# Moving the causal convolution of a hybrid block: 8 of 31 taps on TensorE as 32x32 diagonal blocks behind the attention heads, 23 on VectorE begun by channel pairs

## The reference

```python
h = rms_norm(x, mix_norm)
a, g, q, k, v, fl = jnp.split(h @ w_in, splits, axis=-1)      # 512 each, fl: 8
# convolution part, 512 channels
u = a * jax.nn.sigmoid(g)
y = depthwise causal convolution of u with 31 taps + conv_b
y_conv = silu(layer_norm(y))
# attention part: 8 heads of 64, with a decay from log_sigmoid(fl)
p = softmax(q k^T / 8 + cum[i] - cum[j], masked to j <= i)
y_attn = p v
x = x + concat(rms_norm(y_conv), rms_norm(y_attn)) @ w_out
```

## Time and profile before

| | |
|---|---|
| median of 3 runs | 1214.56 us (1214.38 to 1214.64) |
| the profiled execution | 1214.71 us, span 1213.0 us |
| granted TensorE clock | 0.999 of full speed (2.4 GHz) |
| PE busy | 1200.2 us (99%), 6271 matmuls |
| DVE busy | 783.7 us (65%) |
| ACT busy | 618.3 us (51%) |
| POOL busy | 66.6 us (5%) |
| first mixer, from a in rows to the start of `mix_out` | 194.0 to 286.7 us in the span |

### The profile page before, as it was taken

How to read it: one execution, slowest core, us unless ns; L and a number is a source line. 1 busy time by engine, 2 the same in 40 slices (tenths; PEclk the granted TensorE clock), 3 DMA queues, 4 the chain that set the end, 5 groups by cost and what they waited for, 6 DMA issues and landing times.

```text
span 1213.0 us, 15892 instructions
## 1 busy us (share of the span) xinstructions
PE 1200.2 (99%) x6271; PEld 1023.7 (84%) x6271; DVE 783.7 (65%) x940; ACT 618.3 (51%) x792; POOL 66.6 (5%) x130
## 2 busy tenths in 40 slices
PE   8999999999999999999999999999999999999998
PEld 6888888998888888899998888888888888888886
DVE  4766546797655554778887755564678666565545
ACT  5544426675544443565744544543556755445333
POOL 1000002002000000200001000000014000000000
PEclk9999999999999999999999999999999999999999
DMA  8987764451587765545302587775365437886630
GB/s 272 314 282 252 237 209 154 153 189 43 174 279 236 257 227 190 186 161 175 123 1 70 164 280 250 242 251 192 138 210 200 147 116 242 255 258 228 230 137 35
DMA packets 172306, 235.32 MB, mean 194 GB/s; under 512 B 13800, under 2 KB 127560, under 8 KB 172232
## 3 DMA queue, kind: packets, MB, share of 16 engines
q1 hardware_dynamic: 172232, 234.30, 59.4%
HBM read 221.67 MB, written 12.58 MB: 193 GB/s over the span
## 4 chain that ended last, share of the span: by engine, by line
PE 90%; DVE 7%; ACT 1%; POOL 1%; DMA 0%; issue 0%; SPq 0%; DVEq 0%; ACTq 0%; POOLq 0%
PE bank L1656 27%; PE bank L1658 27%; PE bank L1657 27%; DVE y L1202 3%; DVE wlo L1085 2%; PE bank L1690 1%; PE bank L2070 1%; PE bank L2085 1%; PE bank L2028 1%; PE bank L2021 1%; PE bank L2093 1%; DMA raw<-in_ffn_w_dram 0%; PE bank L2190 0%; PE bank L2212 0%; PE bank L2177 0%
## 5 line engine op out<-in xcount | busy, mean ns | idle before, releaser
L1085 DVE TENSOR_TENSOR wlo<-raw,whi 128x2048 fp32r<-128x2048 f32 (+1 forms) x190 | 416.1, 2194 | 242.6 <-ACT whi L438 242.6
L438 ACT ACTIVATE whi<-raw 128x2048 fp32r<-128x2048 f32 x190 | 363.0, 1915 | 222.2 <-PE bank L1658 213.4
L1656 PE MATMUL bank<-whi,xThi 128*128 128x512 f32 x1024 | 402.0, 393 | 2.7 <-DVE xTlo L1598 1.3
L1658 PE MATMUL bank<-whi,xTlo 128*128 128x512 f32 x1024 | 399.0, 390 | 0.0
L1657 PE MATMUL bank<-wlo,xThi 128*128 128x512 f32 x1024 | 398.6, 389 | 0.0
L1656 PEld LDWEIGHTS bank<-whi,xThi 128*128 128x128 f32 x1024 | 192.3, 188 | 43.5 <-DVE xTlo L1598 2.0
L1658 PEld LDWEIGHTS bank<-whi,xTlo 128*128 128x128 f32 x1024 | 192.2, 188 | 40.1
L1657 PEld LDWEIGHTS bank<-wlo,xThi 128*128 128x128 f32 x1024 | 192.4, 188 | 39.0
L1656 PE MATMUL bank<-whi,hThi 128*128 128x512 f32 x352 | 137.3, 390 | 0.0
L1658 PE MATMUL bank<-whi,hTlo 128*128 128x512 f32 x352 | 137.0, 389 | 0.0
L1657 PE MATMUL bank<-wlo,hThi 128*128 128x512 f32 x352 | 137.0, 389 | 0.0
(11 more groups left out here) (411 smaller groups left out, 1083.9 us busy)
## 6 DMA issues: line engine op xcount, KB each, us to landing
raw<-in_ffn_w_dram SPq DMA_DIRECT2D x176, 256.0 KB, 4.3
raw<-in_ffn_w_in_dram SPq DMA_DIRECT2D x176, 256.0 KB, 4.1
raw<-in_ffn_w_dram SPq DMA_DIRECT2D x22, 1024.0 KB, 5.3
raw<-in_ffn_w_out_dram SPq DMA_DIRECT2D x22, 1024.0 KB, 5.3
raw<-in_gdn_w_in_dram SPq DMA_DIRECT2D x16, 1024.0 KB, 5.3
hidden<-hblk SPq DMA_DIRECT2D x44, 256.0 KB, 5.3
hraw<-hidden SPq DMA_DIRECT2D x176, 64.0 KB, 3.3
raw<-in_w_in_dram SPq DMA_DIRECT2D x10, 1024.0 KB, 5.2
```

Of the source, the lines that this page charges most:

```text
L438: act.activation(whi[w % SPLIT][:], raw[w % RAW][:], ACT.Copy).then_inc(w_hi, 1)
L1085: dve.tensor_tensor(wlo[w % SPLIT][:, c], raw[w % RAW][:, c], whi[w % SPLIT][:, c].bitcast(F32), ALU.subtract).then_inc(w_lo, 1)
L1656: pe.matmul(psum, lhs[0], rhs[0], start=start, stop=False, skip_group_check=True)
L1658: return pe.matmul(psum, lhs[1], rhs[0], start=False, stop=stop, skip_group_check=True)
```

## The change

It does these things together:

- The first four slots of `w_in` hold columns of a and g by channel pairs (two tiles of 128 channels): slots s and s+1 the 256 columns of a and of g for pair 0, slots s+2 and s+3 those of pair 1 (`stream_pairs`, four transfers of 256 KB for a slot in place of one of 1 MB). PE forms pair 0 in rows and transposes a and g of it ahead of pair 1, which it forms in columns. The sigmoid and u are made for each pair on its own, and DVE begins the taps of pair 0 while PE is at pair 1.
- DVE has 23 taps in place of 25, in steps of one tap and one pair.
- The other 8 taps go to PE as blocks of 32 x 32 of the diagonal: 8 taps x 4 channel tiles x 4 row groups are 128 matmuls of 32 x 32 by 256 columns, each channel tile with a bank of its own (4 to 7). Row group r of channel tile c writes column group (r+c) mod 4. They stand behind all heads (`conv_taps`); no tap is left between the steps of a head. DVE makes the blocks with one multiplication by `eye32`; ACT's 24 diagonal matrices are gone.
- ACT copies these four banks to `y_pe`, and PE adds them to banks 0 and 1 with eight more products, by identities that are turned by 32 c columns. This copy stands ahead of the table load for Silu and of the squares of the attention output in ACT's list.
- One mask product of 256 columns for a head in place of two of 128.
- DVE's splits: five stand before the heads (up to slot s+12) and none within them; slot s+13 is converted behind the heads, on ACT ahead of the copies and on DVE behind the scaling of the attention output.

```diff
+    def stream_pairs(name, w):
+        v = w[:, 0:2 * DC].rearrange("(k p) (g n) -> p k g n", p=P, g=2)
+        for m in range(2):
+            for h in range(2):
+                slots.append([(("k", k), v[:, 4 * h + k, :, m * 256:(m + 1) * 256]) for k in range(4)])
...
 ACT
+                act.preload_act_table(ACT.Sigmoid)
+                def gate(m):
+                    return act.activation(gs[:, 2 * m:2 * m + 2, :]..., bank[1 + 2 * m][:], ACT.Sigmoid)
+                act.wait_ge(*once("m_aT"))
+                gate(0).then_inc(did("m_sig0"), 1)
...
                 for h in range(H1 + 2):
-                    if h == 3:
-                        split(s + 10 + SPLIT)
...
+                split(s + 10 + SPLIT)
+                act.wait_ge(*once("c_taps"))
+                for c in range(CT):
+                    ins = act.activation(y_pe[:, c, :], bank[4 + c][:, 0:SEQ], ACT.Copy)
+                ins.then_inc(did("c_taps_in"), 1)
                 act.preload_act_table(ACT.Silu)
...
 DVE
+                split(s + 1 + SPLIT)
+                dve.wait_ge(*once("m_zero_u"))
+                dve.tensor_tensor(diag[:], <8 taps x 4 tiles, broadcast over 32>, <eye32, broadcast>, ALU.mult)
+                gated_pair(0)
+                convolve_pair(0, 3)
+                split(s + 2 + SPLIT)
+                convolve_pair(0, 3)
                 split(s + 3 + SPLIT)
+                convolve_pair(0, EARLY - 6)
+                dve.wait_ge(*once("m_sig1"))
+                gated_pair(1)
                 split(s + 4 + SPLIT)
-                convolve(2)
+                convolve_pair(1, 4)
...
-                for i, n in enumerate((4, 3, 2, 2)):
+                for i, n in enumerate((4, 3, 1, 0, 0)):
                     convolve(n)
                     split(s + 5 + i + SPLIT)
                 for h in range(H1):
...
-                    if h not in (0, 2):
-                        convolve(1)
-                    if h in (2, 5):
-                        split(s + 9 + h // 5 + SPLIT)
+                    convolve_next()
                 dve.wait_ge(sem("at_exp"), H1)
                 step(dve.reciprocal(rinv[:], rsum[:]))
-                convolve(2)
+                convolve(1)
...                          (two scalings of yA by 1/sum, the rest of the taps, two by rms and gain)
+                split(s + 10 + SPLIT)
                 dve.wait_ge(sem("m_rows"), 48)
...
 PE
-                block_cols(s + 2, xT, [bank[2], bank[3]])
                 pe.wait_ge(*once("m_a"))
                 ...transposes...
+                block_cols(s + 2, xT, [bank[2], bank[3]])
...
-                        ins = pe.matmul(S_[:, d], ident_r[:], mask_r[:], ...)
+                    diagonal = S_[:].rearrange("p (t c) -> p t c", t=2)[:, :, 0:P]
+                    pe.matmul(diagonal, ident_r[:], mask_r[:].unsqueeze(1).broadcast_to([P, NT, P]), ...)
...
-                    if 3 <= i <= H1 + 1:
-                        conv_tap(i - 1)
...
+                def conv_taps():
+                    for k in range(PE_TAPS):
+                        at = TAPS - PE_TAPS + k
+                        for c in range(CT):
+                            for r in range(4):
+                                q, to = slice(32 * r, 32 * r + 32), 32 * ((r + c) % 4)
+                                pe.matmul(bank[4 + c][to:to + 32, 0:SEQ], diag[q, CT * k + c, :], u[q, c, at:at + SEQ],
+                                          start=k == 0, stop=k == PE_TAPS - 1)
+                conv_taps()
+                wait for c_conv0, c_conv1
                 for t in range(NT):
                     for c in range(CT):
                         pe.matmul(bank[t][:, c * P:(c + 1) * P], y[:, c, t * P:(t + 1) * P], ident[:], ...)
+                pe.wait_ge(*once("c_taps_in"))
+                for t in range(NT):
+                    for c in range(CT):
+                        ins = pe.matmul(bank[t][:, c * P:(c + 1) * P], y_pe[:, c, t * P:(t + 1) * P], turned[:, 32 * c:32 * c + P], ...)
                     ins.then_inc(sem("c_T"), 1)
                     pe.wait_ge(sem("a_in"), t + 1)
                     ...transposes of yA...
```

More of the change, by code:

```diff
@@ L45, in build_program @@
     WARM = 11
-    PE_TAPS = 6
+    PE_TAPS = 8
+    EARLY = 8
     SLOT = 4 * 512
@@ L545, in mixer1 @@
                 act.activation(flT[:], bank[6][0:2 * H1, 0:SEQ], ACT.Copy).then_inc(did("m_flT"), 1)
[L547 to L552, removed]
+                act.preload_act_table(ACT.Sigmoid)
+                def gate(m):
+                    return act.activation(gs[:, 2 * m:2 * m + 2, :].rearrange("p c t -> p (c t)"), bank[1 + 2 * m][:], ACT.Sigmoid)
+                act.wait_ge(*once("m_aT"))
+                gate(0).then_inc(did("m_sig0"), 1)
                 split(s + 2 + SPLIT)
-                act.wait_ge(*once("m_tap"))
-                diagonals(range(PE_TAPS // 2)).then_inc(did("m_diag0"), 1)
                 split(s + 3 + SPLIT)
                 act.wait_ge(w_used, s + 4)
-                for i in range(2):
-                    ins = act.activation(gs[:, 2 * i:2 * i + 2, :].rearrange("p c t -> p (c t)"), bank[2 + i][:], ACT.Sigmoid)
-                ins.then_inc(did("m_sig"), 1)
+                gate(1).then_inc(did("m_sig1"), 1)
                 split(s + 4 + SPLIT)
@@ L1190, in mixer1, with convolve_pair @@
                 s = first["mix"]
[L1191 to L1196, removed]
+                taps = [0, 0]
+                def convolve_pair(m, n):
+                    until = min(taps[m] + n, TAPS - PE_TAPS)
+                    for k in range(taps[m], until):
+                        for i in range(2):
+                            c = 2 * m + i
                             src = u[:, c, k:k + SEQ]
@@ L1207, in mixer1 @@
-                split(s + 3 + SPLIT)
[L1208 to L1214, removed]
+                            ins.then_inc(sem(f"c_conv{m}"), 1)
@@ new lines, in convolve_pair, with convolve_next, convolve, gated_pair @@
+                    taps[m] = until
+                def convolve_next():
+                    convolve_pair(0 if taps[0] <= taps[1] else 1, 1)
+                def convolve(n):
+                    for i in range(2 * n):
+                        convolve_next()
+                def gated_pair(m):
+                    dve.tensor_tensor(u[:, 2 * m:2 * m + 2, PAD:], bank[2 * m][:].rearrange("p (c t) -> p c t", c=2),
+                                      gs[:, 2 * m:2 * m + 2, :], ALU.mult).then_inc(did(f"m_u{m}"), 1)
+                    dve.wait_ge(*once(f"m_u{m}"))
@@ new lines, in mixer1 @@
+                split(s + 1 + SPLIT)
+                dve.wait_ge(*once("m_zero_u"))
+                dve.tensor_tensor(diag[:], tap[:, TAPS - PE_TAPS:TAPS, :].rearrange("p k c -> p (k c)").unsqueeze(2)
+                                  .broadcast_to([P, CT * PE_TAPS, 32]),
+                                  eye32[:, 0:32].unsqueeze(1).broadcast_to([P, CT * PE_TAPS, 32]), ALU.mult).then_inc(did("m_diag"), 1)
+                dve.wait_ge(*once("m_sig0"))
+                dve.wait_ge(*once("m_aT"))
@@ L1884, in mixer1 @@
                 ins.then_inc(did("m_cumT"), 1)
-                pe.wait_ge(*once("m_sig"))
+                pe.wait_ge(*once("m_sig1"))
+                pe.wait_ge(*once("m_u1"))
                 block_rows(s + 8, xT, [bank[2], bank[3]])
@@ L1893, in scores @@
                         c = slice(0, P) if t == 0 else slice(P, 384)
-                        d = slice(0, P) if t == 0 else slice(2 * P, 384)
                         pe.matmul(S_[:, c], qz[:, h, t * P:(t + 1) * P], kz[:, h, 0:P * (t + 1)], start=t == 0, stop=False,
                                   skip_group_check=True)
[L1897 to L1907, removed]
+                    diagonal = S_[:].rearrange("p (t c) -> p t c", t=2)[:, :, 0:P]
+                    pe.matmul(diagonal, ident_r[:], mask_r[:].unsqueeze(1).broadcast_to([P, NT, P]), start=False, stop=True,
+                              skip_group_check=True).then_inc(sem("at_S"), 1)
+                def conv_taps():
+                    pe.wait_ge(*once("m_diag"))
+                    for k in range(PE_TAPS):
[3 more added lines that the diff above has]
+                                q, to = slice(32 * r, 32 * r + 32), 32 * ((r + c) % 4)
+                                ins = pe.matmul(bank[4 + c][to:to + 32, 0:SEQ], diag[q, CT * k + c, :], u[q, c, at:at + SEQ],
+                                                start=k == 0, stop=k == PE_TAPS - 1, skip_group_check=True)
+                    ins.then_inc(did("c_taps"), 1)
                 pe.wait_ge(*once("m_k"))
@@ L1935, in mixer1 @@
                         pe.matmul(bank[3][:, o], pT1[:, h % 2, 2 * P:], v1[:, 1, o], start=False, stop=True).then_inc(sem("at_pv"), 1)
-                for n in range(H1 + 1, NT * PE_TAPS):
-                    conv_tap(n)
-                pe.wait_ge(sem("c_conv"), CT * (TAPS - PE_TAPS))
+                conv_taps()
+                for m in range(2):
```

(13 more changed lines are left out.)

31 lines of the change are left out of this document (17 added, 14 removed).

## The result

The changed kernel takes 1219.01 us (median of 8 runs) and the kernel before 1214.47 beside it: ratio 1.0033, interval 1.0023 to 1.0042, slower by 4.5 us. Its executions lie in two groups, 1217.4 to 1217.6 and 1219.0 to 1219.3; the profiled one (1218.96, span 1217.2) is of the second. The forecast was 1216.0, and slower by over 0.2% had 37 in 100.

A forecast was written before the change was run, and what follows sets the result against it. PE bounds the kernel, except DVE's stretch before `mix_out`. 6.5 us won in the heads and 7.9 lost behind them put `mix_out` 1.4 later: 1214.71 + 1.4 − .15 = 1216.0 us; range 1212.4 to 1220.6.

The forecast's parts named there:

- The sign of the gain against the loss: Up to `mix_out`: 6.5 us won in the heads, 7.9 lost behind them, so 1.4 us later.
- the links of the tail: After PE's taps: four copies 1.25, table load 1.28, squares .72 and .63, POOL's factors, DVE's scaling, split 2.2, xTlo.
- rival 1: PE's taps: the 16 tiles run only in part, taps take 5.5 to 9 us, 1217.1 to 1220.6; 22 in 100.
- Start and heads: Before the taps: DVE free at 257.0; PE leaves the heads at 273.6, from 14.0 work and 3.3 waits, 6.5 earlier.
- DVE behind the heads: After the heads: two yA products and four taps, 1.2 + 1.6; last tap ends near 276.7, 6.6 us earlier.
- The taps: PE's 8 taps behind the heads: all 16 tiles at once, 4.4 us plus .4 for the last record, ending at 278.4.
- The prediction's sign of being wrong, over 6 us: PE's taps: if they took over 6 us, the forecast would be wrong.
- The tail: From the end of PE's taps to `mix_out`: 9.7 us, so `mix_out` begins at 288.1 against 286.71.
- Behind `mix_out`: From the start of `mix_out` on: PE sets the time again.
- Rival 2: PE's taps: only four tiles at a time, taps 15.4 us, `mix_out` 12.4 later, 1227.0 us; 14 in 100.
- Rival 3: Heads: ACT and DVE return each in time, PE leaves at 270.3 to 271; 1212.7 to 1213.4 us; 10 in 100.
- Rival 4: Tail: last split and table load are not on the way, 3.5 us less, 1212.5; 6 in 100 with the unseen.

The follow-up runs named there:

- split first: Changed kernel with VectorE's split of slot s+13 right behind its last tap, ahead of the attention output's scalings: 1216.27 us.
- half the columns: Changed kernel with every TensorE tap matmul on 128 instead of 256 columns, output not the reference's: 1216.46 us in one execution.
- four tiles: Changed kernel without the rotation, row group r writing column group r, so only the 4 diagonal tiles are used: 1226.66 us in one execution.
- the version with 7 and 8 spare matmuls: Changed kernel plus unread matmuls on TensorE: 7 ahead of the wait for the first scaling, 8 behind the last yA transposes: 1217.43 us.

## Why the prediction came out as it did

The sign of the gain against the loss, the mechanism and the links of the tail were right. The time was inside the range, but 3.0 us above the forecast: the range reaches so far up for rival 1, and about half of the 3.0 is the clock, which no rival had.

- *Start and heads*: right in the total, in part by luck. PE leaves the heads at 273.76 (forecast 273.6), and DVE, which waits 0.32 for PE ahead of 257.10, is free at 256.8 (forecast 257.0). PE's three long waits for ScalarE (0.89, 0.49, 0.56) come to 1.9 where 1.3, 0.6 and 0.8 were worked out; PE's busy time comes to 15.7 where 14.0 and 0.6 of short waits were. The errors partly cancel. One of them is the mask product: a head's scores take 0.83 and not 0.78. Of what the heads won, that product is only 0.25; that the rest comes from the taps leaving them is argued from the sum, and no run changes that alone.
- *DVE behind the heads*: right, 276.74 for 276.7. It then idles for 7.3 us, not for some 4; the prediction's own links give 6.
- *The taps*: the term that was mis-sized. 4.8 us with the last record were forecast, 6.04 measured (279.80 − 273.76). Two things in it: a round of 16 costs 0.31 and not the 0.24 read from L1975, and there is a gap behind record 218. That is rival 1, whose band starts at 1217.1, but by a sum and not by a doubling: some 0.1 for the 16 records on top of 0.2 for the columns. The prediction's sign of being wrong, over 6 us, is just met. The Trainium skill (TensorE: Matmul & The Clock Gate, Part 3: Packing small matmuls) gave 5.8 by its factor of 10.6, an estimate; 6.04 measured, or 5.7 to the start of the last record with 0.15 of a gap in it, is nearer to that than to my 4.4.
- *The tail*: right. From the end of the taps to `mix_out` 9.6 us, forecast 9.7; VectorE's second scaling begins 5.7 behind the taps (forecast 5.8); and moving the squares took 4.6 of it away.
- *Behind `mix_out`*: missed altogether. The prediction took PE to set the time again from there at the old pace. The tail left PE idle, the clock fell, 1.6 us. With the 1.2 of the taps this is nearly all of the 3.0, and both went the same way. The times of the lower group agree with the slower taps alone: 1216.0 and 1.24 are 1217.2.
- *Rival 2* (four at a time) is false: within 0.14 us of the first start 16 records are under way, four row groups of each bank, and the pace agrees: 512 columns take 0.23 in `mix_out`, so four row groups in turn over 256 columns would need some 0.45 a round, an estimate, where 0.31 was measured. The Trainium skill (TensorEngine Tiling (Array Packing), Restrictions and Gotchas, PSUM Pressure) says that different row tiles can't use one bank at the same time; this trace disagrees as long as they write different partitions of it (PE by stretches of 0.05 us, this line alone, below), and it decides.
- *Rival 3* (heads at PE's floor) is false: 273.76 and not 271. *Rival 4* (split and table load not on the way) is false: both stand in the chain.

```profile
273.85:273.90 0.05, 0.05 (x16) 1.00 0.00 0
```

What stays open: whether the gap in the taps is a late supply of PE's instructions, as its distance from the instruction transfer suggests. Also open is why the same idle stretch of 2.2 us took the clock at once in three kernels (split first, half the columns, four tiles) and in the changed kernel's profile only after a second one. Taps inside the heads, which would need two channel tiles in one bank and the same partitions, were not tried.

## What to carry to other kernels

When a piece of work is moved to another engine's end, read which instructions of the other engines' lists stand behind its result without needing it: here a table load, two squares and a split, 4.6 us, more than the change itself lost. A wait put into an in-order list wants everything that is ready placed ahead of it. And if a tail leaves TensorE idle for some 2 us, as here, price the stretch behind it at either level of the clock. The balance between two engines (7 taps, not 8) gave 0.7 us once that order was right; on the old order it was not tried.

## What the hardware showed

- The granted clock fell to 0.50 for over 3 us in a stretch where PE was fully busy, after it had stood idle for 2.2 and 2.4 us with 2.1 us of work between; in three other kernels it fell behind the first 2.2 us alone; in the version with 7 and 8 spare matmuls, where the waits were 0.6 us each, it stayed at 1.00.
- Sixteen tiles of 32 x 32 run at once, four row groups into one bank, each at other partitions. A round of 16 matmul records over 256 columns costs 0.31 us and over 128 columns 0.21; four tiles cost 0.21 a round of four.
- The gap in the taps: PE idle for 0.15 to 0.53 us in the versions with sixteen tiles and whole columns, 1.23 with half the columns, and none with four tiles at a time. PE goes on 2.3 to 2.7 us behind the begin of a 16 KB transfer on the instruction queue.
